# Four row tiles ahead of all weights, norm weight rows read from HBM, late row tiles through GpSimd's queue

## The chip, the cores and the metric

The kernel runs on the 8 cores of one Trainium2 chip. Every core runs the same program on its own data: one prompt of 2048 rows and 16 of the 128 sample rows. The metric is the device time in microseconds of the slowest core. TensorE (PE) multiplies, VectorE (DVE), ScalarE (ACT) and GpSimd (POOL) compute element by element, SyncE (SP) only issues transfers. GpSimd and ScalarE can issue transfers as well.

## The reference, cut to what matters

```
h = rmsnorm(x, g_mix);  proj = h @ w_in                # 1024 -> 3584 columns
a = proj[:, 0:512];  z = gelu(proj[:, 512:1536])       # z = u | v
gate_a, gate_b = sigmoid(proj[:, 1536:2560]), sigmoid(proj[:, 2560:3584])
pa = pool_mixer(a)     # per 128 columns: sums over windows of 2, 4, 8, 16 rows, mean - a, @ w_pool, * s_pool
v  = rmsnorm(v, g_v);  s = tril(w_s) @ v (chunks of 128 rows) + b_s;  sg = u * s
x  = x + (gate_a * (pa @ w_pool_out) + gate_b * (sg @ w_gmlp_out)) @ w_out
h2 = rmsnorm(x, g_ffn); x = x + (silu(h2 @ w_gate) * (h2 @ w_up)) @ w_down
y  = rmsnorm(x, g_final)
```

The outputs are y, the last 15 rows of a, the pool state of the samples, and v of the samples.

## The kernel before

The 2048 rows of a core are 16 row tiles of 128 rows and 1024 float32 columns (512 KB each in HBM), and the 16 sample rows are a 17th. They are read into the buffer X by `xload` (L614). All weights are packed into units of 128 x 1024 float32 values, 512 KB each in HBM. `load_unit` (L593) reads them through GpSimd's queue, which casts them to float16 on the way, into the ring buffer.

`norm` (L705) makes the normalised row tile. ScalarE squares and sums the rows, GpSimd raises the sum to the power -1/2 (L696), and VectorE (for tiles 0 and 1 half of it ScalarE) writes the float16 tile into hb, a buffer for two tiles. The tile is then transposed into hT. Tiles 0 to 7 are transposed on PE (L734) and copied out of PSUM; tiles 8 to 15 and the sample rows go by a transposing transfer on SP's queue (L722). With `late=True` (tiles 0 to 3) the tile is scaled by the row's factor alone and g_mix is multiplied in when it is copied out of PSUM, from its transposed form gT. Otherwise one VectorE instruction multiplies by factor and by gmix, g_mix repeated in all partitions.

The first part of the kernel, which alone is changed, runs over four blocks b of 512 rows (L870). A block has `a_stage` (L758, 4 groups of 128 columns), `chain` (L772, VectorE's window sums), `v_tile` (L811, one per row tile, with a norm of its own), and `u_stage` (L833, which also has the spatial product). It uses 12 weight units: a (4), v (4), u (4). Then follow the gates, the output product, and the two feed-forward parts, which are not changed.

The rows g_mix, g_v and b_s are needed in all 128 partitions. Before, they come as one row of 2048 values (`rowc`, L623), and PE repeats them by four float32 products with a row of ones, after which ScalarE and VectorE copy them out of PSUM into gmix, gv and bs_rep.

The order of the work on each engine is written by a planner, `schedule` (L232). It simulates the engines with a duration for each instruction and takes, for each engine, the operation that can start first, and among those the one with the lowest priority number. Transfers have a model of their own, `Traffic` and L301 to L311: a rate for each queue and a lead and a tail. The order is fixed when the program is built; on the chip every engine goes through its list in order, and waits on semaphores. `after=[...]` on a transfer makes it wait until another transfer has landed or another operation has ended. After planning, L1369 to L1392 fill gaps of PE's plan in the first 30 us with products that nobody reads (L1385, called filling products here).

Of the kernel before, what the change touches and what calls it, by code (L numbers as in the profile page):

```python
# [34 lines left out]
C_ID = 0  # L35
C_GT = C_ID + 128
C_STB = C_GT + 8
C_WS = C_STB + 1024
# [7 lines left out]
C_B0 = C_W00 + 4  # L46
C_GF = C_B0 + 4
C_GN = C_GF + 1024
C_ALL = C_GN + 1024

# [48 lines left out]
class Traffic:  # L99
# [9 lines left out]
    def steps(self, t, pend, until):  # L109
        while True:  # L110
            act = [q for q in pend if pend[q] and pend[q][0][1] <= t]
            nxt = min([x[0][1] for x in pend.values() if x and x[0][1] > t], default=float('inf'))
            rate = {q: (340.0 if t < 60000.0 else 300.0) if len(act) == 1 else (self.EARLY if t < 18000.0 else self.LATE)[q] for q in act}
            for q in act:
                nxt = min(nxt, t + pend[q][0][2] / rate[q])
            nxt = min(nxt, until)
            if nxt == float('inf'):
                return t
            for q in act:
                pend[q][0][2] -= (nxt - t) * rate[q]  # L120
# [21 lines left out]
class Prog:  # L142
# [89 lines left out]
    def schedule(self, bank_free0):  # L232
# [32 lines left out]
        while nleft:  # L265
# [35 lines left out]
            if o.dma is not None:  # L301
                if o.xbar:
                    o.done = o.end + 1900.0
                elif o.eng == 'act' and o.start < 20000.0:
                    o.done = o.end + 4100.0
                elif o.nbytes < 16384:
                    o.done = o.end + 3500.0
                elif o.eng == 'pool':
                    flow.add(o, 'pool', o.end, max(1600.0, 4900.0 - o.end), 900.0)
# [99 lines left out]
def build_nc():  # L409
    nc = bass.Bass("TRN2", target_bir_lowering=False)  # L410

    def din(name, shape):
        return nc.dram_tensor(name, list(shape), F32, kind="ExternalInput").ap()
# [20 lines left out]
    with es:  # L434
        def sb(name, shape, dt):
            return es.enter_context(nc.sbuf_tensor(name, list(shape), dt))
# [8 lines left out]
        junk = sb("junk", [128, XW], F16)  # L445
        idg = sb("idg", [128, 136], F32)
        ident_b = sb("ident_b", [128, 128], F16)
        wsbs = sb("wsbs", [128, 1024], F16)
        csm = sb("csm", [128, 80], F32)
        NCOL = 76  # L450
# [66 lines left out]
        def pt_():  # L517
            return PT()
# [94 lines left out]

        def xload(t, after=(), prio=None):  # L614
            prio = -10.0 + 0.1 * t if prio is None else prio
            if t < NT:
                o_ = dma('sp', X[:, XR(t), 0:D], xp[t * 128:(t + 1) * 128, :], 'x%d' % t, 524288, prio, after)
            else:
                o_ = dma('sp', X[:NSMP, XR(t), 0:D], xs[:, :], 'x%d' % t, 65536, prio, after)
# [19 lines left out]

        def cload(dst, c0, n, sem, prio, after):  # L640
            dma('sp', dst, cst[:, c0:c0 + n], sem, n * 512, prio, after=[after])
# [14 lines left out]
        memset('dve', AB[:, :, 0:32], 0.0)  # L656
        memset('dve', ones1[:, :], 1.0)
        vcopy(ident_b[:, :], ident_f[:, :], -5, 128)
        act(stmp[:, 0:1], mhalf[:, 0:1], AF.Square, -8.5)
        for j, (dst, nm) in enumerate(((gmix[:, 0:512], 'act'), (gmix[:, 512:1024], 'dve'), (gv, 'dve'),  # L660
                                       (bs_rep[:, :, :].rearrange("p g i -> p (g i)"), 'dve'))):
            pt = pt_()
            pr = -3.0
            mm(pt, lambda p: p[:, :], [(ones1[0:1, :], grow[0:1, 512 * j:512 * j + 512])], pr)
            if nm == 'act':
                act(dst, PV(pt, lambda p: p[:, :]), AF.Copy, pr)
            else:
                vcopy(dst, PV(pt, lambda p: p[:, :]), pr, 512, per=1.04)

# [35 lines left out]
        def norm(t, grep, prio, xbar=True, two=False, dst=None, late=False):  # L705
# [4 lines left out]
            if late:  # L710
                hw = 512 if t < 2 else 0
                if hw:
                    act(hbs[hi][:R, 0:hw], X[:R, XR(t), 0:hw], AF.Copy, prio, scale=r)
                ho = vts(hbs[hi][:R, hw:D], X[:R, XR(t), hw:D], r, None, ALU.mult, ALU.bypass, prio, D - hw)
            elif two:
                act(hbs[hi][:R, :], X[:R, XR(t), 0:D], AF.Copy, prio, scale=r)
                ho = vtt(hbs[hi][:R, :], hbs[hi][:R, :], grep[:R, :], ALU.mult, prio, D, per=0.52)
            else:
                ho = vstt(hbs[hi][:R, :], X[:R, XR(t), 0:D], r, grep[:R, :], ALU.mult, ALU.mult, prio, D)
            dst = hT[:, :, t * 128:t * 128 + R] if dst is None else dst  # L720
            if xbar:
                P.add('sp', lambda e: e.dma_start_transpose(out=dst, in_=hbs[hi][:R, :]),  # L722
                      reads=[hbs[hi][:R, :]], writes=[dst], dur=1220.0, lat=0.0, prio=-20.0,
                      dma='t%d' % hi, nbytes=330000).xbar = True
                return ho
            for h in range(2):
# [805 lines left out]
```

How the kernel before makes its waits and increments, by code:

```python
    def run(self, eng, e, sems):  # L391
        for o in self.order[eng]:
            for (sk, val) in o.waits:
                e.wait_ge(sems[sk], val)
            ins = o.fn(e)
            if o.dma is not None:
                ins.then_inc(sems[o.dma], 16)
            else:
                ins.then_inc(sems['E_' + eng], 1)
# [1008 lines left out]
            @block.sync  # L1408
            def _(e):
                P.run('sp', e, sems)
                for key in ('o0', 'o1', 'o2', 'o3', 'o4', 'o5', 'o6', 'q0', 'q1', 'q2', 'q3'):
                    e.wait_ge(sems[key], P.cnt[key])
```

## Time and profile before

| | |
|---|---|
| median of 3 runs | 757.73 us (757.55 to 758.4) |
| profiled execution | 757.22 us, span of its slowest core (core 0) 755.6 us |
| spans of cores 0 to 7 | 755.6, 754.2, 754.4, 754.2, 752.2, 753.8, 751.9, 754.4 us |
| PE busy | 739.2 us, 98% of the span |
| DVE, ACT, POOL busy | 548.6, 362.3, 98.7 us |

Times within the trace are microseconds from the start of the span. A row of the timeline has the start, the duration, the engine, the line, the operation, output and inputs, the shape, the count of instructions merged, and in brackets the idle time before and what ended it. A busy PE includes the filling products.

### The profile page before, as it was taken

What the parts mean: (1) busy time and instruction counts of PE and PEld (TensorE: products, weight loads), DVE (VectorE), ACT (ScalarE), POOL (GpSimd) and SP (SyncE); (2) the same over time, 40 slices, a digit from 0 to 9 for tenths busy, and PEclk for the clock granted to TensorE, in tenths of its full rate; (3) what the DMA queues carried; (4) which work ended last, traced back from release to release, by engine and by line L of the source; (5) the groups of instructions that cost most, each with busy time, mean ns of one, the idle gap of its engine ahead of it and who ended that gap; (6) DMA issues with size and microseconds to landing.
All of it is one profiled execution on the core that took longest, in us unless ns stands there. A gap on an engine that the chain in (4) does not pass through costs nothing.

```text
span 755.6 us, 14731 instructions; the slowest of 8 cores (751.9 to 755.6 us)
## 1 busy us (share of the span) xinstructions
PE 739.2 (98%) x4808; PEld 436.7 (58%) x4808; DVE 548.6 (73%) x1119; ACT 362.3 (48%) x788; POOL 98.7 (13%) x173
## 2 busy tenths in 40 slices
PE   8899899999999999999999999999999999999995
PEld 4554355666666664445666666666666654444543
DVE  3779898777777665787767676777667698766665
ACT  4695446454444446675555555555555521121212
POOL 3243232000000002222001000000000300000000
PEclk9999999999999999999999999999999999999998
DMA  8995437232313239677994232333222870623332
GB/s 191 207 293 80 58 60 121 36 43 54 43 29 40 59 95 266 112 117 104 230 270 83 42 46 41 56 64 50 43 43 43 110 185 2 221 89 137 130 97 112
DMA packets 53643, 77.46 MB, mean 103 GB/s; under 512 B 28736, under 2 KB 29120, under 8 KB 53551
## 3 DMA queue, kind: packets, MB, share of 16 engines
q0 software_dynamic: 15840, 28.84, 25.9%
q1 hardware_dynamic: 37294, 47.29, 22.1%
q8 instruction: 40, 0.66, 0.4%
q10 hardware_dynamic: 434, 0.38, 0.2%
q14 instruction: 35, 0.29, 0.1%
HBM read 82.04 MB, written 17.40 MB: 132 GB/s over the span
## 4 chain that ended last, share of the span: by engine, by line
PE 89%; DVE 3%; DMA 2%; issue 2%; ACT 2%; POOL 1%; SPq 0%; DVEq 0%; ACTq 0%; POOLq 0%
PE ps L529 87%; DMA X<-xp 1%; DMA hT<-hb 1%; PE ps L1070 1%; ACT junk L551 1%; PE ps L1385 1%; DVE hb L566 1%; POOL rs L696 1%; DVE actr L561 1%; PE ps L734 0%; ACT Fb L551 0%; DVE mrg L788 0%; DVE actr L566 0%; PE ps L848 0%; SPq L585 0%
## 5 line engine op out<-in xcount | busy, mean ns | idle before, releaser
L529 PE MATMUL ps<-hT,ring 128*128 128x384 f16 (+6 forms) x1428 | 231.9, 311 | 4.1 <-DMA hT<-hb 2.3
L561 DVE TENSOR_TENSOR Fb<-Fb,ps 128x344 f32<-128x344 f32 (+3 forms) x299 | 154.5, 531 | 52.0 <-PE ps L529 24.7
L529 PEld LDWEIGHTS ps<-hT,ring 128*128 128x128 f16 x1428 | 132.7, 98 | 83.0 <-issue 9.3
L551 ACT ACTIVATE Fb<-ps 128x384 f32<-128x384 f32 (+4 forms) x245 | 114.8, 475 | 122.7 <-PE ps L529 99.1
L561 DVE TENSOR_TENSOR X<-X,ps 128x512 f32<-128x512 f32 (+6 forms) x157 | 84.6, 546 | 53.1 <-PE ps L529 35.2
L551 ACT ACTIVATE Fb<-Fb 128x384 f32<-128x384 f32 (+2 forms) x174 | 85.9, 494 | 69.3 <-DVE Fb L561 67.4
L529 PE MATMUL ps<-actr,ring 128*128 128x344 f16 (+2 forms) x600 | 108.9, 309 | 0.1
L585 POOL DMA_DIRECT2D ring<-wpk x93 | 50.0, 545 | 310.3 <-PE ps L529 288.2
L529 PE MATMUL ps<-ring,mrg 128*128 128x512 f16 x360 | 81.4, 379 | 0.0
L529 PEld LDWEIGHTS ps<-actr,ring 128*128 128x128 f16 x600 | 57.5, 98 | 30.6 <-issue 0.5
L551 ACT ACTIVATE junk<-X 128x1025 f16<-128x1025 f32 (+3 forms) x40 | 41.5, 1038 | 46.8 <-DVE X L561 43.4
L529 PE MATMUL ps<-actr 128*128 128x384 f16 (+2 forms) x336 | 63.9, 324 | 0.0
L529 PEld LDWEIGHTS ps<-ring,mrg 128*128 128x128 f16 x360 | 35.1, 98 | 41.5 <-issue 0.4
L529 PE MATMUL ps<-actr,hb 128*128 128x384 f16 (+2 forms) x280 | 54.6, 319 | 0.0
L696 POOL TENSOR_TENSOR rs<-ss,mhalf 128x1 f32<-128x1 f32 (+1 forms) x51 | 39.0, 765 | 116.8 <-ACT junk L551 113.7
L529 PE MATMUL ps<-hT,X 128*128 128x512 f16 (+3 forms) x238 | 51.4, 338 | 0.0
L551 ACT ACTIVATE X<-ps 128x344 f32<-128x344 f32 (+2 forms) x87 | 38.1, 442 | 26.8 <-PE ps L529 23.1
L529 PE MATMUL ps<-hT,actr 128*128 128x384 f16 (+2 forms) x220 | 47.2, 337 | 0.0
L529 PEld LDWEIGHTS ps<-actr 128*128 128x128 f16 x336 | 32.8, 98 | 21.3 <-issue 0.2
L551 ACT ACTIVATE junk<-Fb 128x513 f16<-128x513 f32 (+2 forms) x25 | 19.2, 769 | 40.4 <-DVE Fb L561 36.8
L529 PEld LDWEIGHTS ps<-actr,hb 128*128 128x128 f16 x280 | 27.4, 98 | 16.2
L529 PE MATMUL ps<-hT,hb 128*128 128x384 f16 (+3 forms) x188 | 36.5, 321 | 0.0
(178 smaller groups left out, 795.0 us busy)
## 6 DMA issues: line engine op xcount, KB each, us to landing
ring<-wpk POOLq DMA_DIRECT2D x93, 256.0 KB, 4.8
X<-xp SPq DMA_DIRECT2D x25, 512.0 KB, 7.4
x1d<-X SPq DMA_DIRECT2D x16, 512.0 KB, 13.0
Fb<-x1d SPq DMA_DIRECT2D x8, 512.0 KB, 4.1
yp<-Fb SPq DMA_DIRECT2D x8, 512.0 KB, 2.8
hT<-wpk POOLq DMA_DIRECT2D x8, 256.0 KB, 11.6
X<-x1d SPq DMA_DIRECT2D x4, 512.0 KB, 4.3
actr<-x1d SPq DMA_DIRECT2D x4, 512.0 KB, 3.9
```

The costliest lines, as they stand in the source:

```text
L529: ins = e.matmul(out=ap, lhsT=l, rhs=rr, start=(start and i == 0), stop=(stop and i == len(pairs) - 1), skip_group_check=skip)
L551: return e.activation(out=P.r(out), in_=P.r(in_), func=func, scale=scale, **kw)
L561: return P.add(eng, lambda e: e.tensor_tensor(out=P.r(out), in0=P.r(a), in1=P.r(b), op=op), reads=[a, b], writes=[out], dur=vdur(n, per), ...
L566: return P.add('dve', lambda e: e.scalar_tensor_tensor(out=P.r(out), in0=P.r(a), scalar=sc, in1=P.r(b), op0=op0, op1=op1), reads=rd, write ...
L585: return P.add(q, lambda e: e.dma_start(out=out, in_=in_), reads=[in_], writes=[out], dur=(560.0 if q == 'pool' else 400.0), lat=0.0, prio ...
L696: P.add('pool', lambda e: e.tensor_tensor(out=rs[:R, k:k + 1], in0=ss[:R, k:k + 1], in1=mhalf[:R, 0:1], op=ALU.pow), reads=[ss[:R, k:k + 1 ...
L1070: ins = e.matmul(out=o_, lhsT=l, rhs=r, start=(m_ == 0), stop=(m_ == len(terms[dd]) - 1))
L1385: ins = e.matmul(out=PS[7][:, :], lhsT=z[:, 512:640], rhs=z[:, 0:512], start=True, stop=True)
```

## The change

- Only the four row tiles 0 to 3 are issued at once on SP's queue; all a and v units wait until row tile 1 has landed.
- g_mix, g_v and b_s are stored in HBM repeated 128 times and are read by transfers (1 MB in all); the four products, their copies and `rowc` are gone. b_s is cast by one VectorE copy.
- The causal mask comes first on GpSimd's queue; gT moves into csm.
- Row tiles 8 to 11 wait for unit u1 only and stay on SP's queue. Row tiles 12 to 15, the sample rows and the constants of the samples (C_STB, C_WP, C_SEL) move to GpSimd's queue, behind row tile 9 or 11.
- Tiles 4 to 7 are normalised with `late=True`. Where `late` is set, VectorE now does the whole scaling and both halves of the copy out of PSUM, which ScalarE shared before.
- The planner's rates, leads and tails for transfers are altered, and the filling products are counted from 0.95 us on instead of 2.0 us.

```diff
-            rate = {q: (340.0 if t < 60000.0 else 300.0) if len(act) == 1 else ...
+            rate = {q: (300.0 if not 8000.0 < t < 60000.0 else 340.0) if len(act) == 1 else ...
...
-                    o.done = o.end + 1900.0
+                    flow.add(o, 'sp', o.end, 100.0, 1070.0)
...
-                    flow.add(o, 'sp', o.end, 1300.0, 900.0)
+                    flow.add(o, 'sp', o.end, 1300.0, 1200.0 if 600.0 < o.end < 3000.0 else 900.0)
...
-        dma('act', idg[:, :], cst[:, C_ID:C_ID + 136], 'c0', 69632, -10.1)
-        dma('act', grow[0:1, 0:2048], rowc[:, :], 'c1', 8192, -10)
-        dma('act', csm[:, 0:76], cst[:, C_SM:C_SM + 76], 'c3', 38912, -8.95)
-        for t in range(2):
+        for t in range(4):
             xload(t)
-        for t in range(2, 4):
-            xload(t)
+        dma('act', ident_f[:, :], cst[:, C_ID:C_ID + 128], 'c0', 65536, -10.1)
+        dma('act', csm[:, 0:84], cst[:, C_SM:C_SM + 84], 'c3', 43008, -10.0)
+        dma('pool', mask, cst[:, C_MASK:C_MASK + 128], 'c7', 65536, -11.0)
         wd_ = {}
         for g in range(4):
-            wd_[('a', g)] = load_unit(('a', g), 8 + g, 0.1 + 0.01 * g)
+            wd_[('a', g)] = load_unit(('a', g), 8 + g, 0.1 + 0.01 * g, [x_dma[1]])
         for k in range(4):
-            wd_[('v', k)] = load_unit(('v', k), k, 0.2 + 0.01 * k)
+            wd_[('v', k)] = load_unit(('v', k), k, 0.2 + 0.01 * k, [x_dma[1]])
...
-        cload(mask, C_MASK, 128, 'c7', -9.63, wd_[('a', 3)])
-        cload(mrg[:, o + 1536:o + 2048], C_WS, 512, 'c8', -9.62, wd_[('v', 0)])
-        cload(mrg[:, o + 512:o + 1536], C_STB, 1024, 'c9', -1, wd_[('u', 3)])
-        cload(mrg[:, o + 2048:o + 2560], C_WP, 512, 'c10', -1, wd_[('u', 3)])
-        cload(mrg[:, o + 2560:o + 2688], C_SEL, 128, 'c11', -1, wd_[('u', 3)])
-        for t in range(4, 12):
-            if t not in x_dma:
-                xload(t, after=[wd_[('u', 1 if t < 8 else 2)]])
+        cload(mrg[:, o + 1536:o + 2048], C_WS, 512, 'c8', -9.26, wd_[('v', 3)])
+        cload(gv, C_GM + 1024, 512, 'c1', -9.25, wd_[('v', 3)])
+        cload(bs_raw, C_GM + 1536, 512, 'c12', -9.24, wd_[('v', 3)])
+        cload(gmix, C_GM, 1024, 'c13', -9.05, wd_[('u', 1)])
+        for t in range(8, 12):
+            xload(t, after=[wd_[('u', 1)]])
...
-        memset('dve', ones1[:, :], 1.0)
...
-        for j, (dst, nm) in enumerate(((gmix[:, 0:512], 'act'), (gmix[:, 512:1024], 'dve'), (gv, 'dve'),
-                                       (bs_rep[:, :, :].rearrange("p g i -> p (g i)"), 'dve'))):
-            ...
-            mm(pt, lambda p: p[:, :], [(ones1[0:1, :], grow[0:1, 512 * j:512 * j + 512])], pr)
-            ...
+        vcopy(bs_rep[:, :, :].rearrange("p g i -> p (g i)"), bs_raw, 7.5, 512)
...
-                hw = 512 if t < 2 else 0
-                if hw:
-                    act(hbs[hi][:R, 0:hw], X[:R, XR(t), 0:hw], AF.Copy, prio, scale=r)
-                ho = vts(hbs[hi][:R, hw:D], X[:R, XR(t), hw:D], r, None, ALU.mult, ALU.bypass, prio, D - hw)
+                ho = vts(hbs[hi][:R, :], X[:R, XR(t), 0:D], r, None, ALU.mult, ALU.bypass, prio, D)
...
-                    if h:
-                        for k in range(4):
-                            act(dst[:, 4 + k, :], PV(pt, ...), AF.Copy, prio, scale=gT[:, 4 + k, :], n=R)
-                    else:
-                        vtt(dst[:, 0:4, :], src, gT[:, 0:4, :].to_broadcast([128, 4, R]), ALU.mult, prio, 4 * R)
+                    vtt(dst[:, 4 * h:4 * h + 4, :], src, gT[:, 4 * h:4 * h + 4, :].to_broadcast([128, 4, R]), ALU.mult, prio, 4 * R)
...
-                    h_op[t] = norm(t, gmix, base - 95.0 + 0.1 * (t % 4), xbar=b > 1)
+                    h_op[t] = norm(t, gmix, base - 95.0 + 0.1 * (t % 4), xbar=b > 1, late=b < 2)
             if b == 1:
                 for t in range(12, NT):
-                    xload(t, after=[h_op[t - 8]])
+                    xload(t, after=[h_op[t - 8], x_dma[9]], prio=0.5 + 0.01 * t, q='pool')
+                cload(mrg[:, o + 512:o + 1536], C_STB, 1024, 'c9', 0.7, x_dma[11], q='pool')
+                cload(mrg[:, o + 2048:o + 2560], C_WP, 512, 'c10', 0.71, x_dma[11], q='pool')
+                cload(mrg[:, o + 2560:o + 2688], C_SEL, 128, 'c11', 0.72, x_dma[11], q='pool')
                 if b == 1:
-                    xload(NT, after=[h_op[7]])
+                    xload(NT, after=[h_op[7], x_dma[9]], prio=0.49, q='pool')
...
-        t_ = 2000.0
+        t_ = 950.0
...
-                n_ = int((gap - 200.0) / (300.0 if t_ < 5000.0 else 235.0)) if gap > 700.0 else 0
+                n_ = int((gap - 200.0) / (420.0 if t_ < 2000.0 else 235.0)) if gap > 700.0 else 0
```

## Rows read from the trace of the kernel before

**Rows 1.** Busy us of each engine (instructions) by stretch, core 0; then granted clock, DMA share, GB/s.
```profile
20.00:40.00 20.00, 17.93 (x141) 11.04 (x139) 15.81 (x39) 12.97 (x35) 7.40 (x10) 1.00 0.92 222
...
36.90:124.00 87.10, 84.21 (x507) 41.87 (x505) 75.00 (x133) 52.20 (x116) 30.89 (x41) 0.98 0.59 118
...
160.00:240.00 80.00, 80.00 (x551) 53.69 (x549) 59.18 (x130) 39.80 (x89) 5.30 (x10) 1.00 0.26 40
```
**Rows 2.** Timeline of PE, core 0.
```profile
5.93 5.48 PE L529 MATMUL ps<-Fb,mrg 1*128 1x512 f32 x6
11.34 1.03 PE L734 MATMUL ps<-ident_b,hb 128*128 128x128 f16 x8
...
28.79 5.34 PE L529 MATMUL ps<-ring,hT 128*128 128x512 f16 x24
...
36.87 1.89 PE L529 MATMUL ps<-ring,hT 128*128 128x512 f16 x8
...
78.20 8.75 PE L529 MATMUL ps<-hT,ring 128*128 128x512 f16 x32 [2.30 <-DMA hT<-hb]
...
124.08 0.39 PE L848 MATMUL ps<-wsbs,mrg 128*128 128x128 f16 x4
```
**Rows 3.** Timeline of PE, core 7: first products of tile 4, last spatial products.
```profile
38.04 1.89 PE L529 MATMUL ps<-ring,hT 128*128 128x512 f16 x8
...
122.60 0.39 PE L848 MATMUL ps<-wsbs,mrg 128*128 128x128 f16 x4
```
**Rows 4.** Timeline of PE, core 6: the same two, and the a products of block 2.
```profile
34.63 1.89 PE L529 MATMUL ps<-ring,hT 128*128 128x512 f16 x8
...
74.35 7.07 PE L529 MATMUL ps<-hT,ring 128*128 128x512 f16 x32 [0.80 <-DMA hT<-hb]
...
121.67 0.39 PE L848 MATMUL ps<-wsbs,mrg 128*128 128x128 f16 x4
```
**Rows 5.** Row tile 1 and unit a0: ns of the issue, its start, us from issue to landing.
```profile
L585 SPq DMA_DIRECT2D X<-xp x1: 412/412/412, 1.5 to 1.5; - x1
DMA to landing us min/median/max: 5.8/5.8/5.8
...
L585 POOL DMA_DIRECT2D ring<-wpk x1: 664/664/664, 1.5 to 1.5; - x1
DMA to landing us min/median/max: 10.4/10.4/10.4
```
**Rows 6.** The same for unit v3 and for unit u0.
```profile
L585 POOL DMA_DIRECT2D ring<-wpk x1: 587/587/587, 5.3 to 5.3; - x1
DMA to landing us min/median/max: 20.0/20.0/20.0
...
L585 POOL DMA_DIRECT2D ring<-wpk x1: 577/577/577, 28.8 to 28.8; - x1
DMA to landing us min/median/max: 5.2/5.2/5.2
```
**Rows 7.** Chain of waits, core 0, start, length, what: row tile 11, the last of blocks 0 to 2.
```profile
44.23 10.79 DMA X<-xp
```
**Rows 8.** Waits of SP's queue in the first 100 us: total, times, longest.
```profile
SPq L394 <- DVE hb L566: 41.3, 11, 9.0
```
**Rows 9.** VectorE in norm: combined form, scaling alone, the two copies out of PSUM (min/median/max ns).
```profile
L566 DVE SCALAR_TENSOR_TENSOR hb<-X,rs,mrg 128x1024 f16<-128x1024 f32 x10 | 12.7, 1279 | 2.7 <-DMA hT<-hb 1.9 <-POOL rs L696 0.8
...
16.24 0.75 DVE L572 TENSOR_SCALAR hb<-X,rs 128x1024 f16<-128x1024 f32 x1
...
L577 DVE COPY hT<-ps x4: 418/421/424, 36.2 to 43.0; 128x512 f16<-128x512 f16 x4
...
L561 DVE TENSOR_TENSOR hT<-ps,idg x4: 692/692/693, 12.5 to 22.0; 128x512 f16<-128x512 f16 x4
```
**Rows 10.** Timeline of POOL: a root beside an idle VectorE, and one beside a busy one.
```profile
14.37 0.55 POOL L696 TENSOR_TENSOR rs<-ss,mhalf 128x1 f32<-128x1 f32 x1 [5.08 <-ACT junk L551]
...
36.89 1.32 POOL L696 TENSOR_TENSOR rs<-ss,mhalf 128x1 f32<-128x1 f32 x1 [1.60 <-ACT junk L551]
```

More of the change, by code:

```diff
@@ L35 @@
 C_ID = 0
-C_GT = C_ID + 128
-C_STB = C_GT + 8
+C_STB = C_ID + 128
 C_WS = C_STB + 1024
@@ L46 @@
 C_B0 = C_W00 + 4
-C_GF = C_B0 + 4
+C_GT = C_B0 + 4
+C_GF = C_GT + 8
 C_GN = C_GF + 1024
-C_ALL = C_GN + 1024
+C_GM = C_GN + 1024
+C_ALL = C_GM + 2048
 def unit_list():
@@ L112, in steps @@
             nxt = min([x[0][1] for x in pend.values() if x and x[0][1] > t], default=float('inf'))
-            rate = {q: (340.0 if t < 60000.0 else 300.0) if len(act) == 1 else (self.EARLY if t < 18000.0 else self.LATE)[q] for q in act}
+            rate = {q: (300.0 if not 8000.0 < t < 60000.0 else 340.0) if len(act) == 1 else (self.EARLY if t < 18000.0 else self.LATE)[q] for q in act}
             for q in act:
@@ L308, in schedule @@
                 elif o.eng == 'pool':
-                    flow.add(o, 'pool', o.end, max(1600.0, 4900.0 - o.end), 900.0)
+                    flow.add(o, 'pool', o.end, max(1600.0, 5000.0 - o.end), 900.0)
                 else:
-                    flow.add(o, 'sp', o.end, 1300.0, 900.0)
+                    flow.add(o, 'sp', o.end, 1300.0, 1200.0 if 600.0 < o.end < 3000.0 else 900.0)
             else:
@@ L445, in build_nc @@
         junk = sb("junk", [128, XW], F16)
-        idg = sb("idg", [128, 136], F32)
+        ident_f = sb("ident_f", [128, 128], F32)
         ident_b = sb("ident_b", [128, 128], F16)
         wsbs = sb("wsbs", [128, 1024], F16)
-        csm = sb("csm", [128, 80], F32)
+        csm = sb("csm", [128, 84], F32)
         NCOL = 76
@@ L612, in build_nc, with xload @@
         x_dma = {}
-        def xload(t, after=(), prio=None):
+        def xload(t, after=(), prio=None, q='sp'):
             prio = -10.0 + 0.1 * t if prio is None else prio
             if t < NT:
-                o_ = dma('sp', X[:, XR(t), 0:D], xp[t * 128:(t + 1) * 128, :], 'x%d' % t, 524288, prio, after)
+                o_ = dma(q, X[:, XR(t), 0:D], xp[t * 128:(t + 1) * 128, :], ('x%d' if q == 'sp' else 'y%d') % t, 524288, prio, after)
             else:
-                o_ = dma('sp', X[:NSMP, XR(t), 0:D], xs[:, :], 'x%d' % t, 65536, prio, after)
+                o_ = dma(q, X[:NSMP, XR(t), 0:D], xs[:, :], ('x%d' if q == 'sp' else 'y%d') % t, 65536, prio, after)
             x_dma[t] = o_
-        dma('act', idg[:, :], cst[:, C_ID:C_ID + 136], 'c0', 69632, -10.1)
-        dma('act', grow[0:1, 0:2048], rowc[:, :], 'c1', 8192, -10)
-        dma('act', csm[:, 0:76], cst[:, C_SM:C_SM + 76], 'c3', 38912, -8.95)
-        for t in range(2):
+        for t in range(4):
             xload(t)
-        for t in range(2, 4):
-            xload(t)
+        dma('act', ident_f[:, :], cst[:, C_ID:C_ID + 128], 'c0', 65536, -10.1)
+        dma('act', csm[:, 0:84], cst[:, C_SM:C_SM + 84], 'c3', 43008, -10.0)
+        dma('pool', mask, cst[:, C_MASK:C_MASK + 128], 'c7', 65536, -11.0)
         wd_ = {}
         for g in range(4):
-            wd_[('a', g)] = load_unit(('a', g), 8 + g, 0.1 + 0.01 * g)
+            wd_[('a', g)] = load_unit(('a', g), 8 + g, 0.1 + 0.01 * g, [x_dma[1]])
         for k in range(4):
-            wd_[('v', k)] = load_unit(('v', k), k, 0.2 + 0.01 * k)
+            wd_[('v', k)] = load_unit(('v', k), k, 0.2 + 0.01 * k, [x_dma[1]])
         xg = {4: ('v', 1), 5: ('v', 1), 6: ('v', 2), 7: ('v', 3)}
@@ L638, in build_nc, with cload @@
             wd_[('u', g)] = load_unit(('u', g), 4 + g, 0.3 + 0.01 * g, [x_dma[4 + g]])
-        def cload(dst, c0, n, sem, prio, after):
-            dma('sp', dst, cst[:, c0:c0 + n], sem, n * 512, prio, after=[after])
-        cload(mask, C_MASK, 128, 'c7', -9.63, wd_[('a', 3)])
-        cload(mrg[:, o + 1536:o + 2048], C_WS, 512, 'c8', -9.62, wd_[('v', 0)])
-        cload(mrg[:, o + 512:o + 1536], C_STB, 1024, 'c9', -1, wd_[('u', 3)])
-        cload(mrg[:, o + 2048:o + 2560], C_WP, 512, 'c10', -1, wd_[('u', 3)])
-        cload(mrg[:, o + 2560:o + 2688], C_SEL, 128, 'c11', -1, wd_[('u', 3)])
-        for t in range(4, 12):
-            if t not in x_dma:
-                xload(t, after=[wd_[('u', 1 if t < 8 else 2)]])
+        def cload(dst, c0, n, sem, prio, after, q='sp'):
+            dma(q, dst, cst[:, c0:c0 + n], sem, n * 512, prio, after=[after])
+        cload(mrg[:, o + 1536:o + 2048], C_WS, 512, 'c8', -9.26, wd_[('v', 3)])
[4 more added lines that the diff above has]
+            xload(t, after=[wd_[('u', 1)]])
         zm = memset('dve', actr[:, 0, 1408:2048], 0.0, -6.0)
@@ L723, in norm @@
                       reads=[hbs[hi][:R, :]], writes=[dst], dur=1220.0, lat=0.0, prio=-20.0,
[L724 removed]
+                      dma='t%d' % hi, nbytes=250000).xbar = True
                 return ho
@@ L1521 @@
             "xp": x_prompt[c], "xs": np.ascontiguousarray(x_sample[c * NSMP:(c + 1) * NSMP, 0, :]),
-            "st": stc, "cst": cc, "rowc": rowc, "wpk": wpk,
+            "st": stc, "cst": cc, "wpk": wpk,
         })
```

17 lines of the change are left out of this document (3 added, 14 removed).

## The prediction

> **What bounds the kernel now.** I read the busy time by stretch first. From 160 to 240 us PE is busy for all of its time at granted clock 1.00 [rows 1], and so, but for a few us, up to the end. What happens before about 125 us is therefore passed on one to one: whatever time PE's last spatial product of block 3 gains, the kernel gains. I take that product as the landmark. It stands at 124.08 us on core 0, which is the slowest [rows 2], at 122.60 on core 7 [rows 3] and at 121.67 on core 6 [rows 4]. From there to the end of the span are 755.6 - 124.1 = 631.5, 754.4 - 122.6 = 631.8 and 751.9 - 121.7 = 630.2 us.
>
> Then the timeline of PE, for what delays the landmark. The reader is to see two marks. The products of row tile 4 (the first of block 1) start at 36.87 on core 0, when the a and v products of block 0 are done. The a products of block 2 start at 78.20 after 2.30 us of waiting for a transposed row tile, and their 32 products then take 8.75 us, where core 6 needs 7.07 [rows 2, 4]: 1.7 us more, with a lower granted clock after the wait.
>
> Does a gain at the first mark reach the landmark? The cores answer that. Core 7 comes to its first mark at 38.04, 3.4 us behind core 6 (34.63), but to the landmark only 0.9 us behind [rows 3, 4]. From mark to landmark are 87.2 us on core 0, 87.0 on core 6 and 84.6 on core 7. An early start is mostly eaten by something that stands at a fixed time. The chain of waits names it: row tile 11, issued at 44.23, landing at 55.0 [rows 7], and from it the squares, roots, scaling and transposing transfers to the wait at 78.20. So there are two limits: the start of block 1, and the arrival of row tiles 8 to 11. The transfer engines are full meanwhile (share 0.92 from 20 to 40 us, [rows 1]), and SP's queue waited 41.3 us for VectorE [rows 8]: in its order tiles 12 to 15 stand ahead of 8 to 11, behind the scaling of tiles 4 to 7.
>
> **The change part by part.** *Row products.* Eight float32 records go; the first six stand from 5.93 to 11.34, ahead of the first transposes [rows 2]. Their place is empty then, not used: the a products need unit a0, which now waits for tile 1. That landed at 1.5 + 5.8 = 7.3 us [rows 5]; with 0.6 us of issue and u0's 5.2 us to landing [rows 6], a0 lands at 13.1 instead of 1.5 + 10.4 = 11.9 [rows 5]. The later seven units took (25.3 - 11.9)/7 = 1.9 us each before, with two row tiles beside them (v3: 5.3 + 20.0 = 25.3, rows 5, 6). At the rate below 524 KB alone in the queues take 1.9 us too, or 1.6 if that rate contains gaps. So v3 lands between 24.3 and 26.4: 25 us, unchanged. Tiles 2 and 3 come earlier and their norms are then over when weights land; the a products (block 0: 7 us) run as units arrive, and the v products of block 0, done at 34.0 before [rows 2], end about 1.7 us after v3, at 27.
>
> *The first mark.* It needs tile 4 in hT. Tile 4 still waits for v1 and lands near 27.7 (before: at u0's issue at 28.8, rows 6, at the latest). Square 1.25, root 0.55 plus hand-over, scaling 0.75 [rows 9, 10], transposes and copy: 5 us. Mark at 32.6, or 31 to 35. That is 4.3 us earlier on core 0, 2.0 on core 6, 5.4 on core 7. By the least remainder of [rows 3], 84.6 us, the landmark follows at 117.2; by the greatest, 87.2, at 119.8.
>
> *The second limit.* Up to the landing of tile 11, 16 row tiles, 12 units (524 KB each) and 0.44 MB of constants were read: 15.1 MB in the 53.9 us since 1.1 us, 0.28 MB per us. Now tiles 12 to 15 are behind (-2.10 MB) and the repeated rows are ahead (three of 262 KB with the spatial weights, gmix 524 KB; 1.05 MB more than before): 14.07 MB, so tile 11 lands at 1.1 + 50.2 = 51.3, 3.7 us earlier. If tiles 12 and 13 on the other queue share with 10 and 11, 1.05 MB or 3.7 us come back and nothing is gained; if the queues run without the hole that SP's waits leave, 2 us more are gained. I take 3.7, the price of the bytes. The wait at 78.20 moves to 74.5; from there to the landmark are 124.1 - 78.2 = 45.9 us, without the slow clock 44.2: 118.7. If that slow clock comes back, 120.4.
>
> *VectorE.* For each of tiles 4 to 7 a combined form (1.28) and one copy (0.42) become a scaling (0.75) and two products (0.69 each) [rows 9]: +0.43 us, +1.7 for four. In block 0 two halves of scaling and four more copies of 0.69 come from ScalarE, while three copies of the repeated rows go: about +1 us, at a time when VectorE waits for weights anyway. Between the marks VectorE was busy for 75.0 of 87.1 us [rows 1]; now 76.5 of about 86. It has room in the sum but not everywhere, since its order is fixed: nothing at the low end, 1.7 us at the high end. ScalarE's load falls. I put 0.3 us.
>
> *GpSimd's queue.* Nine transfers more at 0.58 us [rows 6] are 5.2 us. It was busy 30.9 of 87.1 us between the marks [rows 1], so they fit. But each waits in line: tiles 12 to 15 for tile 9 and for the scaling of tiles 4 to 7, the constants for tile 11, and the roots of `v_tile` and `norm` stand behind them. Here the planned order must hold; nothing to 8 us, taken as 0. A root of 0.55 us already takes 1.32 while VectorE is busy [rows 10].
>
> The Trainium skill (SBUF — State Buffer, section "Who interferes with whom") says that a DVE copy, cast or `tensor_scalar` in a two-port mode locks the port that GpSimd needs for writing descriptors; it speaks against this change, which makes four more `tensor_scalar` and issues nine more transfers on GpSimd. By that rule each meeting would cost at most one scaling, 0.75 us, some 3 us in all on GpSimd. The trace's issues of 0.58 and 0.59 us show no such wait; the rule alters neither the sum nor a chance.
>
> *The rest.* The filling products move 1 us forward and change only what PE does while it has nothing to do. The mask and gT cost nothing new.
>
> **Sum.** The later of 117.2 to 119.8 and 118.7, with 0.3 us: landmark at 119.0 us, against 124.1 on core 0 and 122.4 on the middle core. With 631.5 us behind it, the span is 750.5; the slower tail of some cores adds 0.3. The profiled execution lay 757.22 - 755.6 = 1.6 us over its span: 752.4. The median of the runs lies 0.5 us over the profiled one: 752.9 us, a gain of 4.8.
>
> **Rivals.** (A) *The added bytes eat it.* Tiles 10 and 11 share with the GpSimd queue, tile 11 lands at 55.0 as before, and the wait at 78.20 stays. Only core 0's lower clock or part of the start is gained, 1 to 2 us: 756.3. For it: the full engines [rows 1]. Against: SP's queue had 41.3 us of waits [rows 8] that tiles 8 to 11 no longer stand behind. The Trainium skill (DMA: Bandwidth & Descriptors, "Issuing engines are not separate DMA queues") says that all queues end on the same 16 engines, so that moving a transfer gains its place in the order only; the trace's share of 0.92 agrees.
>
> (B) *VectorE becomes the bound* between the marks: its added work shows in full and once more in PE's waits for it. 2 to 2.5 us of the gain go: 755.2. For it: busy for 86% of that stretch [rows 1]. Against: core 7 did the same work in 84.6 us.
>
> (C) *GpSimd's queue blocks* (the other side). If tile 9 lands later than planned, the issue of tile 12 holds up every root behind it, VectorE waits for the roots, PE for VectorE. Tile 9 is at 13.0 MB, about 47.6 us by the rate above. Each us of lateness beyond the slack is lost; it decides from 6 us on (the gain of 4.8 and the bound of 1.5 us). With 8 us: 761.
>
> (D) *More is gained*: the first mark at 31 us and no wait at block 2. The landmark at 31 + 84.6 = 115.6: 749.5.
>
> **Chances.** Forecast 0.48 (its own range 751 to 755), A 0.16, B 0.14, C 0.11, D 0.11. What a measurement can tell from no change is 0.2%, 1.5 us, so faster is below 756.2. Of the forecast, B and D all is faster except 0.03; of A a third: 0.75. Same: 0.03 and half of A, 0.13; slower: C and what is left of A, 0.12. The range reaches from D to A's upper end: 749.0 to 757.5.
>
> **What would show it.** First products of tile 4 at 31 to 35 us on all cores. Landing of tile 11 at about 51. The a products of block 2 at about 74.5 with little wait and no lower clock after it. The last spatial product at about 119, all cores within 2 us. 630 to 632.5 us from there to the end. It is wrong if roots on GpSimd stand behind its issues for more than 2 us, if tile 11 lands at 55, or if new waits of PE for VectorE show up between 40 and 120 us. It is also wrong if the stretch behind the landmark changes, for which nothing here speaks.

## The result and the profile after

The changed kernel takes 767.98 us (765.79 to 769.24, 4 runs) against 758.07 us (757.55 to 758.94, 4 runs) of the kernel before: 1.0127 times as long, 95% interval 1.0114 to 1.014, 9.9 us between the medians. The forecast was 752.9 us with a range to 757.5. A ratio with an interval in brackets is below always that of a kernel to the kernel before, measured beside it.

| | before | after |
|---|---|---|
| span of the slowest core | 755.6 us (core 0) | 767.9 us (core 7) |
| last spatial product, cores 0 to 7 | 124.1, 122.6, 122.0, 122.0, 121.8, 122.7, 121.7, 122.6 | 132.5, 131.7, 132.5, 130.4, 128.2, 130.0, 130.2, 136.7 |
| from there to the end of the span | 630.2 to 632.4 us on all cores | 631.2 to 633.0 us on all cores |
| PE, DVE busy | 739.2, 548.6 us | 737.4, 549.7 us |

The stretch behind the landmark has kept its length, to within 1 us. So the loss lies before the last spatial product. Further rows of the kernel after are of core 7 where no other core is named.

The timeline of PE at the two marks and at the landmark (columns as in [rows 2]):

```profile
14.66 1.05 PE L527 MATMUL ps<-hT,ring 128*128 128x128 f16 x16 [2.32 <-DMA ring<-wpk]
...
28.08 3.61 PE L527 MATMUL ps<-ring,hT 128*128 128x512 f16 x16 [1.30 <-DMA ring<-wpk]
...
34.67 1.89 PE L527 MATMUL ps<-ring,hT 128*128 128x512 f16 x8 [0.24 <-DVE hT L559]
...
39.89 5.30 PE L527 MATMUL ps<-hT,ring 128*128 128x512 f16 x16 [2.44 <-DMA ring<-wpk]
...
75.58 0.85 PE L527 MATMUL ps<-hT,ring 128*128 128x16 f16 x16 [5.92 <-ACT mrg L549]
77.60 0.36 PE L527 MATMUL ps<-hT,ring 128*128 128x16 f16 x8 [1.17 <-ACT mrg L549]
78.70 0.36 PE L527 MATMUL ps<-hT,ring 128*128 128x16 f16 x8 [0.74 <-ACT Fb L549]
79.18 3.57 PE L527 MATMUL ps<-ring,hT 128*128 128x512 f16 x8
84.47 1.87 PE L825 MATMUL ps<-wsbs,mrg 128*128 128x128 f16 x16 [1.71 <-ACT junk L549]
86.13 2.79 PE L527 MATMUL ps<-ring,hT 128*128 128x512 f16 x8
...
136.68 0.39 PE L825 MATMUL ps<-wsbs,mrg 128*128 128x128 f16 x4
```

The reader is to see the first products of tile 4 at 34.67, where [rows 3] have 38.04: the early start is there. But from that mark to the landmark are 102.0 us instead of 84.6. Of the 17.4 us more, 10.4 are idle time (12.2 us of waits in the trace, 1.8 before) and about 5 are a lower clock, 1.7 of them at 39.9 us and 3.4 between 79 and 89. Eight 128x512 products take 3.57 and 2.79 us where [rows 2] have 1.89. Sixteen spatial products take 1.87 where the same sixteen take 1.05 in an undisturbed stretch of the first experiment, and the sixteen products at 39.89 take 5.30 against 3.61 at 28.08. The other 1.9 us I can't assign. The windows show the clock in the column behind the brackets of POOL (columns as in [rows 1]):

```profile
40.00:45.00 5.00, 5.00 (x16) 1.90 (x15) 0.84 (x5) 0.60 (x1) 0.00 (x0) 0.66 0.90 153
60.00:65.00 5.00, 5.00 (x25) 2.29 (x24) 0.09 (x1) 1.23 (x3) 1.55 (x3) 1.00 1.13 98
65.00:70.00 5.00, 4.66 (x22) 1.93 (x20) 0.00 (x0) 0.85 (x1) 0.00 (x0) 1.00 1.10 208
75.00:80.00 5.00, 2.27 (x35) 1.49 (x36) 5.00 (x9) 5.00 (x12) 1.74 (x3) 0.50 0.25 47
```

From 60 to 70 us VectorE stands still while PE still runs on what it has, and from 75 to 80 us PE itself is busy less than half of the time at 0.50 (1.2 GHz). The timeline of VectorE names the wait, and the chain of waits (start, length, what) names what is behind it:

```profile
58.82 1.27 DVE L564 SCALAR_TENSOR_TENSOR hb<-X,rs,mrg 16x1024 f16<-16x1024 f32 x1
72.11 1.28 DVE L564 SCALAR_TENSOR_TENSOR hb<-X,rs,mrg 128x1024 f16<-128x1024 f32 x1 [12.03 <-DMA hT<-hb]
```
```profile
12.68 9.37 DMA ring<-wpk
22.12 7.69 DMA X<-xp
...
30.34 9.42 DMA ring<-wpk
39.89 5.30 PE ps L527 x16
...
54.19 17.83 DMA hT<-hb
```

Two things stand there. Row tile 4, issued at 22.12, lands at 29.8; unit u0 waits for it, is issued at 30.34 and lands after 9.4 us, not 5.2 as in [rows 6]. And a transposing transfer of SP's queue, issued at 54.2 (row tile 8, which VectorE wrote at 52.8), lands after 17.8 us; hb has room for two tiles and the sample rows are in the other half (58.82 above), so VectorE can't write tile 9. The view of the hT tile on SP's queue shows both transfers that are hit, that of tile 8 and that of the sample rows (columns: ns of the issue, first and last start), first of after, then of the same core before:

```profile
L704 SPq DMA_TRANSPOSE hT<-hb x2: 1142/1234/1325, 54.2 to 60.2; - x2
DMA to landing us min/median/max: 12.5/15.2/17.8
```
```profile
L722 SPq DMA_TRANSPOSE hT<-hb x9: 1217/1232/2017, 56.1 to 84.6; - x9
DMA to landing us min/median/max: 3.1/3.3/4.2
```

What is on the engines meanwhile? GpSimd's queue, with the late tiles (timeline of POOL):

```profile
51.34 0.53 POOL L583 DMA_DIRECT2D X<-xs  x1
...
52.62 0.58 POOL L583 DMA_DIRECT2D X<-xp  x1
53.22 1.32 POOL L681 TENSOR_TENSOR rs<-ss,mhalf 128x1 f32<-128x1 f32 x1
54.51 1.62 POOL L583 DMA_DIRECT2D X<-xp  x3
...
57.29 1.63 POOL L583 DMA_DIRECT2D mrg<-cst  x3
```

How do the two queues share the engines? First the size of the packets. One transposing transfer of a row tile with the engines to itself (ninth experiment below, core 5, DMA view from 54 to 56 us: packets, MB, share of 16 engines):

```profile
q1 hardware_dynamic: 1056, 0.26, 69.2%
```

That is 0.26 MB, a tile of 128 x 1024 values of 2 bytes, in 1056 packets of 256 bytes or less. Now core 4 of the kernel after, from 55 to 60 us, where both queues have work (q0 is GpSimd's, q1 is SP's):

```profile
q0 software_dynamic: 355, 1.30, 91.7%
q1 hardware_dynamic: 357, 0.09, 12.4%
```

GpSimd's queue passes 355 packets of 3.7 KB in the time in which SP's passes 357 small ones. One for one: where packets take turns, a transfer cut into 256-byte packets gets a fifteenth of the bytes. The Trainium skill (DMA: Bandwidth & Descriptors, "Queues, rings and completion order") says that each DMA engine goes round between its queues packet by packet; the counts of this stretch agree.

Turns are not the whole of it. On core 7 the counts are 106 and 618 from 55 to 60 us, and from 58 to 62 us both queues together move only 46 GB/s. In the sixth experiment GpSimd's queue passes 335 packets from 54 to 58 us and SP's none, though a transposing transfer was issued at 53.6. What slows the small packets beyond the turns is not shown by any run.

The collision slows the other side too. ScalarE, which goes through its list in order, waited for row tile 13, which landed at 69.1, 14.6 us after its issue:

```profile
69.14 1.06 ACT L549 ACTIVATE junk<-X 128x1025 f16<-128x1025 f32 x1 [7.92 <-DMA X<-xp]
```

So on core 7 a second path is nearly as late: the root that VectorE needs for its work at 73.32 was done at 71.8, as ScalarE stood behind tile 13. With a short transposing transfer alone this core would have gained only some 1.5 us there (an estimate from these rows). On cores 2 and 3 ScalarE did not wait for a row tile, and VectorE stood still for 9.9 and 9.3 us all the same; of core 2:

```profile
68.16 1.28 DVE L564 SCALAR_TENSOR_TENSOR hb<-X,rs,mrg 128x1024 f16<-128x1024 f32 x1 [9.93 <-DMA hT<-hb]
```

### The profile page after: what moved, and what is told of

Read it like the earlier page. It is cut to its first block, busy times and chain, and to the rows that moved or that the text cites. A ratio compares the mean times of both kernels' runs of the same rounds, so it can differ in the third digit from the quotient of the medians.

```text
span 767.9 us, 14708 instructions; the slowest of 8 cores (760.0 to 767.9 us)
## 1 busy us (share of the span) xinstructions
PE 737.4 (96%) x4812; PEld 435.8 (57%) x4812; DVE 549.7 (72%) x1124; ACT 355.6 (46%) x765; POOL 102.6 (13%) x182
## 4 chain that ended last, share of the span: by engine, by line
PE 87%; DMA 7%; DVE 2%; issue 1%; ACT 1%; POOL 1%; DVEq 0%; SPq 0%; ACTq 0%; POOLq 0%
PE ps L527 85%; DMA ring<-wpk 2%; DMA hT<-hb 2%; DMA X<-xp 2%; PE ps L1050 1%; ACT junk L549 1%; DVE actr L559 1%; PE ps L825 0%; DMA hT<-Fb 0%; POOL rs L681 0%; ACT Fb L549 0%; POOL ring L583 0%; DVE X L559 0%; PE ps L1065 0%; DVE mrg L564 0%
## 5 line engine op out<-in xcount | busy, mean ns | idle before, releaser
L549 ACT ACTIVATE Fb<-ps 128x384 f32<-128x384 f32 (+5 forms) x245 | 115.2, 475 | 128.2 <-PE ps L527 108.5
L549 ACT ACTIVATE Fb<-Fb 128x384 f32<-128x384 f32 (+2 forms) x174 | 85.9, 494 | 69.1 <-DVE Fb L559 67.2
L583 POOL DMA_DIRECT2D ring<-wpk x93 | 51.5, 560 | 323.2 <-PE ps L527 290.2
L681 POOL TENSOR_TENSOR rs<-ss,mhalf 128x1 f32<-128x1 f32 (+1 forms) x51 | 36.5, 716 | 112.8 <-ACT junk L549 111.7
```

Source lines behind the costliest of these rows:

```text
L549: return e.activation(out=P.r(out), in_=P.r(in_), func=func, scale=scale, **kw)
L583: return P.add(q, lambda e: e.dma_start(out=out, in_=in_), reads=[in_], writes=[out], dur=(560.0 if q == 'pool' else 400.0), lat=0.0, prio ...
L681: P.add('pool', lambda e: e.tensor_tensor(out=rs[:R, k:k + 1], in0=ss[:R, k:k + 1], in1=mhalf[:R, 0:1], op=ALU.pow), reads=[ss[:R, k:k + 1 ...
```

## The experiments

Theory 1: the transfers on GpSimd's queue slow the transposing transfers. Theory 2: the added 1 MB of rows delays units and tiles. Theory 3: GpSimd's queue as such is the matter (its own descriptor path, roots behind its issues).

### Late tiles back on SP's queue (e1_sp_queue)

```diff
-  xload(t, after=[h_op[t - 8], x_dma[9]], prio=0.5 + 0.01 * t, q='pool')   # 12 to 15, xs, constants
+  xload(t, after=[h_op[t - 8]])                                            # and constants behind u3
```


> The changed kernel with one part undone: row tiles 12 to 15, the sample rows and the sample constants are back on SP's queue with their old waits. Theory 1 (a transposing transfer on SP's queue takes turns, packet by packet, with the GpSimd queue; the change put 2.9 MB of large packets there just as the transposes of tiles 8 and the sample rows start, and these took 17.8 and 12.5 us instead of about 3): transposing transfers at 3 to 5 us, no 12 us wait of VectorE between 60 and 72 us, median 755 to 759 us, about 10 us under the changed kernel. Theory 2 (the 1 MB more of rows and the later weights cause the loss): the wait moves elsewhere, 764 us or more.

Measured 761.7 us, 1.0052 [1.0035, 1.007]. On its slowest core the transposing transfers were short:

```profile
L707 SPq DMA_TRANSPOSE hT<-hb x5: 1126/1237/1326, 60.7 to 74.8; - x5
DMA to landing us min/median/max: 2.3/3.1/3.2
```

The stall is gone, and 0.75 points of the loss (5.7 us) with it; the landmarks are at 122.6 to 127.1. The time lies between what the two theories expected: 4 us of loss remain. On that core the u units landed at 39.4, 43.3, 45.8 and 48.7 and PE waited at 39.6:

```profile
39.61 3.55 PE L527 MATMUL ps<-hT,ring 128*128 128x512 f16 x8 [3.06 <-DVE wsbs L559]
```

### GpSimd's queue alone (e2_pool_only)

The kernel before, with only tiles 12 to 15, the sample rows and the constants on GpSimd's queue, as in the change.

> The kernel before with that one part of the change alone: tiles 12 to 15, the sample rows and constants on GpSimd's queue, behind tile 9 or 11; weights at once, row products and planner's rates as before. Theory 1: the first transposing transfers meet the same packets, take over 10 us, and the kernel is slower by 6 to 12 us: 764 to 770. Theory 2: no loss, 756 to 759 us, as tiles 8 to 11 are earlier.

Measured 761.46 us, 1.0053 [1.0034, 1.0073]: the sign is right, the size half of what was expected. The longest transposing transfer on the slowest core took 9.7 us and VectorE waited 5.61 us:

```profile
64.63 1.28 DVE L566 SCALAR_TENSOR_TENSOR hb<-X,rs,mrg 128x1024 f16<-128x1024 f32 x1 [5.61 <-DMA hT<-hb]
```

### The same transfers from ScalarE's queue (e3_act_queue)

```diff
-  q='pool'
+  q='act'        # tiles 12 to 15, xs and the three constants
```


> The changed kernel with the same transfers at the same point, but issued from ScalarE's hardware queue instead of GpSimd's. If the loss comes from two queues taking turns by packets (theory 1), the transposing transfers stall as before, over 10 us, 765 to 771 us. If it comes from GpSimd writing descriptors late or being blocked by VectorE (theory 3), they land in 3 to 5 us and the time is 755 to 760 us.

Measured 763.88 us, 1.0083 [1.0059, 1.0107], from two runs: between what the two theories expected. A transposing transfer of 14.2 us is there with no GpSimd in it. The transposing transfers of the slowest core, then the queues from 54 to 62 us (q10 is ScalarE's):

```profile
L704 SPq DMA_TRANSPOSE hT<-hb x5: 1141/1241/1774, 52.0 to 73.2; - x5
DMA to landing us min/median/max: 3.1/3.1/14.2
```
```profile
q10 hardware_dynamic: 774, 2.33, 91.0%
q1 hardware_dynamic: 595, 0.15, 12.2%
```

So a second queue is enough to make such a transfer long, it need not be GpSimd's. But the stall is not the same: the transfers were issued from 48.8 us on, VectorE waited 4.0 us behind the long one and not 12.0, and the engines moved 311 GB/s from 54 to 62 us where core 7 of the changed kernel moved 98 to 107 from 55 to 65. Theory 3 falls for the long transfer; whether GpSimd's queue adds to the stall stays open.

### Rows cut into smaller pieces (e4_small_packets)

The changed kernel, with each tile on GpSimd's queue read as two transfers, of the even and of the odd pieces of 128 columns (512 bytes each in HBM).

> The changed kernel with row tiles 12 to 15 read through GpSimd's queue in pieces of 128 columns (512 bytes) instead of 4 KB rows: the same bytes, eight times the packets if a packet is a piece. Theory 1 (turns by packets): a transposing transfer of 800 packets gets by while 800 small packets pass, some 0.4 MB, so it lands in 4 to 8 us and the time falls to 757 to 763 us. Rival (the bytes or the full engines alone slow them): as the changed kernel or slower, 767 to 772 us.

Measured 762.03 us, 1.0067 [1.0023, 1.0112]; the transposing transfers of the slowest core took 7.6, 8.3 and 10.8 us. But the packets did not become small (and a transposing transfer is 1056 of them, not 800). From 60 to 65 us, core 5:

```profile
q0 software_dynamic: 350, 1.17, 85.3%
```

That is 3.3 KB per packet. The pieces are joined into packets almost as long as before (3.7 KB), so this run can't say whether smaller ones would help. Why the stall was shorter stays open; the starts moved too.

### Rows repeated by PE again, late tiles on SP's queue (e5_sp_and_pe_rows)

The first experiment, with `rowc`, the four float32 products and their copies of the kernel before instead of the 1 MB of repeated rows.

> The changed kernel with two parts undone: late tiles and sample constants on SP's queue, and g_mix, g_v and b_s repeated by PE's four products instead of 1 MB of reads. What is left of the change are the four row tiles ahead of the weights, the scaling of tiles 4 to 7 and the planner's numbers. Theory 2b (the 4 us that stay when the late tiles are back on SP come from the 1 MB, read on SP's queue between 28 and 40 us in turns with the u units, which land at 39.4 to 48.7 us there and at 34.0 to 45.9 before): u0 at about 35, median 754 to 757.5 us. Rival (the late start of the weights or VectorE's added work causes them): 760 to 763 us.

Measured 758.9 us, 1.0007 [0.9993, 1.002]. On its slowest core the u units landed at 37.0, 40.0, 43.2 and 46.7, 2 to 3 us sooner than in the first experiment. That is the second part of the loss, 0.45 points. The time lies between the two expected ranges, and u0 was to land at 35: not all of the delay of the u units is the rows.

### Rows repeated by PE, GpSimd's queue kept (e6_pe_rows)

> The changed kernel with only the rows undone: late tiles stay on GpSimd's queue. If the two losses add up (late tiles 6 us, rows 4 us), 763 to 765 us, with transposing transfers of over 8 us. If the late tiles then land before the first transpose and the stall goes, 757 to 759 us.

Measured 758.89 us, 1.0022 [1.0004, 1.0039]: the lower range, but without its condition, as the stall did not go. On the slowest core tiles 12 to 15 were issued at 47.9 to 51.5 (after: 52.6 to 55.6) and landed by 58.9 (after: 73.4). Tile 12 was 5.7 us ahead of the first transposing transfer (53.6), in the changed kernel 1.6 us (54.2). That transfer took 9.1 us, the second 5.2, both landing some 4 us after tile 15; the later ones took 3.1 to 3.3. VectorE waited 3.05 us:

```profile
L713 SPq DMA_TRANSPOSE hT<-hb x6: 1130/1220/1640, 53.6 to 72.5; - x6
DMA to landing us min/median/max: 3.1/3.2/9.1
```

The same queue and the same bytes on it, 4 us sooner against the transposes: half the transfer time, a quarter of the wait. The parts of the change are not additive.

### Repeated rows from HBM alone (e7_hbm_rows_only)

The kernel before with the repeated rows read from HBM (spatial weights and their order as before) and tiles 4 to 7 scaled late.

> The kernel before with the rows read from HBM, and with tiles 4 to 7 scaled late, as they cannot wait for gmix; weights at once, late tiles on SP's queue. Theory 2b: the u units land 3 to 5 us later, the first a products may start earlier as no row products stand ahead, together 758 to 762 us. Rival (the bytes are free, the row products were the cost, as I predicted): 752 to 756 us.

Measured 758.1 us, 1.0002 [0.999, 1.0014]. The first mark was at 33.7 to 35.8 us, 1 to 3 us sooner than before on six of eight cores, and the time is the same, at the lower edge of what theory 2b expected. Of core 7 mark and landmark:

```profile
34.93 1.24 PE L528 MATMUL ps<-ring,hT 128*128 128x512 f16 x5
...
120.31 0.39 PE L840 MATMUL ps<-wsbs,mrg 128*128 128x128 f16 x4
```

That core gained 2.3 us at the landmark (span 751.1 us). Core 3 reached it only at 125.04 (span 755.9), after waits of 1.15 us for a u unit and 2.55 us for VectorE. Without the collision some cores gain, and the slowest, which sets the time, does not.

### Tiles first alone (e8_tiles_first_only)

```diff
-  wd_[('a', g)] = load_unit(('a', g), 8 + g, 0.1 + 0.01 * g)
+  wd_[('a', g)] = load_unit(('a', g), 8 + g, 0.1 + 0.01 * g, [x_dma[1]])   # the v units too
```


> The kernel before with the a and v units waiting for row tile 1 and nothing else changed. a0 lands at 14.5 us instead of 11.9, v3 about as before. If the late start costs nothing, 757 to 758 us; if it is a part of the loss, 759 to 761 us; if the earlier tiles 2 and 3 help, 755 to 757 us.

Measured 757.84 us, 0.9994 [0.9981, 1.0006]: no difference. The landmarks are at 120.3 to 122.7; seven cores waited 0.3 to 1.6 us for a u unit between 42 and 47 us.

### Late tiles on GpSimd's queue, behind the transposes (e9_behind_transposes)

```diff
-  xload(t, after=[h_op[t - 8], x_dma[9]], prio=0.5 + 0.01 * t, q='pool')
+  xload(t, after=[h_op[t - 8], P.ops[h_op[11].i + 1]], prio=0.5 + 0.01 * t, q='pool')   # the constants too
```
The cut is shortened: these calls also move to block 2 of the program. The sample rows are read as in the change.

> The changed kernel with one thing moved: row tiles 12 to 15 and the constants of the samples stay on GpSimd's queue, but are issued only when the transposing transfer of tile 11 has landed. Theory 1 (the stall is made by packets of another queue that are on the engines at the same time): the transposing transfers of tiles 8 to 11 then take 2 to 5 us each instead of 17.8 and 12.5, VectorE's idle 12 us goes, the landmark falls from 136.7 to 124 to 129 us and the time lies at 758.5 to 763, as with the transfers on SP's queue (761.7); only the transposing transfers of tiles 12 to 15 may wait for their rows. Rival (what costs is that the transfers stand on GpSimd's queue at all: its issues, its cast path, roots held up behind waits): 764 or more, with idle time of VectorE or PE behind roots. The time can also be lost again if tile 12 lands after 85 us.

Measured 762.08 us, 1.0071 [1.005, 1.0093]. With the first experiment this is the run that decides: the changed kernel, the row tiles on GpSimd's queue, only not at that time. The slowest core, 45 to 76 us:

```profile
L704 SPq DMA_TRANSPOSE hT<-hb x5: 1147/1228/1327, 52.9 to 71.5; - x5
DMA to landing us min/median/max: 2.3/3.1/3.2
```

No stall of VectorE is left there. The collision has moved to where the tiles now land: the transposes of tiles 12 and 13 (issued at 83.8 and 86.2, beside weight units) took 5.4 and 3.9 us, and PE waited for one:

```profile
89.36 3.61 PE L527 MATMUL ps<-ring,hT 128*128 128x512 f16 x16 [1.59 <-DMA hT<-hb]
```

The landmark there is at 125.0. What is left of the loss is of the size of the first experiment's, which has the same repeated rows. What the two runs show is that it matters which transfers are in flight together; they don't tell turns by packets from any other way in which one queue can hold up another.

### Tiles first and late scaling, nothing else (e10_tiles_first_late_scaling)

> The kernel before with two parts of the change: a and v units wait for row tile 1, and tiles 4 to 7 are normalised with the row factor alone, g_mix being multiplied in by VectorE on the copy out of PSUM. The rows are still repeated by PE, and everything stays on SP's queue in the order of before. If the early gain at the first mark is worth anything by the time of the last spatial product, 755.5 to 757; if something at a fixed later time eats it, 757.5 to 758.5.

Measured 758.59 us, 1.0019 [1.0005, 1.0033]: not faster. The first mark was at 34.9 to 37.9 us, no sooner than before on most cores.

### Planner's numbers of before (e11_planner_before)

The fifth experiment's kernel with the old rates, leads and tails and the old filling products.

> The changed kernel with SP's queue for the late tiles, the rows repeated by PE (that one took 758.9) and now also the planner's numbers and the filling products of before. What is left of the change: four tiles first, the mask first on GpSimd's queue, tiles 8 to 11 behind unit u1, tiles 4 to 7 scaled late. If the planner's new numbers cost something by themselves, 757.0 to 758.2, faster than 758.9 by 0.7 us or more; if the last us is lost in the order of the tiles, 758.5 to 759.5.

Measured 758.7 us, 1.0013 [1.0002, 1.0024], against 1.0007 with the new numbers: the intervals overlap, the new numbers cost nothing that can be seen. No version beats the kernel before.

## Why the prediction was wrong

**The stretch behind the landmark.** Predicted 630 to 632.5 us, measured 631.2 to 633.0. Right but for 0.5 us on one core, and so the landmark was the right thing to follow.

**The first mark.** Predicted 32.6 (31 to 35), measured 34.67 on core 7 and 31.7 to 34.7 on all. Right in sign and size, though by a longer way: a0 landed at 14.5 us instead of 13.1, v3 at 28.6 instead of 25, row tile 4 at 29.8 instead of 27.7. The wait for tile 1 cost a0 2.6 us instead of 1.2, and the seven units behind it took (28.6 - 14.5)/7 = 2.0 us each where 1.6 to 1.9 had been put.

**GpSimd's queue: "nothing to 8 us, taken as 0".** This is the step that failed. I looked for the harm on GpSimd (roots behind issues) and for bytes, and not at who else has packets on the engines at 54 to 72 us: the transposing transfers of tile 8 and of the sample rows, cut some 15 times finer than the rest. The term measured 5.7 us by the undoing (first experiment, 0.75 points) and 0.53% as the part alone (second). On core 7 it shows as 12.0 us of VectorE's time, and from that 9.5 us of PE's waits (5.92, 1.17, 0.74, 1.71) with the clock at half speed behind them. That it is the meeting in time, and not GpSimd's queue as such, is shown by moving the same transfers in time on the same queue (sixth, which also drops the repeated rows, 9.1 us; ninth, 3.2 us), and that a second queue is enough by the third. The prediction also took it that moving a transfer gains its place in the order only: with the same bytes on the same engines the move cost 5.7 us, so it changes the shares as well. Packet turns as the mechanism rest on counts of the trace (355 to 357 on core 4) that other stretches don't repeat; the run that was to vary the packet size did not vary it. So that step is read from the trace, not shown by an experiment, and it is not the whole.

**That the first mark passes on to the landmark by 84.6 to 87.2 us.** This term was mis-sized too. In the first experiment, which has no stall, the early marks (32.0 to 34.3) are followed by 90.5 to 93.3 us on every core. The prediction named row tile 11 as what eats an early start, but left out the u units, which block 1 needs directly behind its first products. u0 was priced at its old 5.2 us; in the changed kernel it took 9.4 and landed at 39.7, where core 0 before has 34.0. PE waited 2.44 us there and then ran at granted clock 0.66. Taking the repeated rows out again brought u0 2.4 us forward and the time down by 0.45 points (fifth). In experiments 5, 7 and 8 the remainder is 85 to 90 us, near the old one; but there the marks come only about 1 us earlier (34 to 37 us against 34.6 to 38.0), and the slowest core gains nothing. No combination of the parts that ran was faster than the kernel before, let alone by 4.8 us.

**The second limit.** Tile 11 was to land at 51.3 by the bytes, 3.7 us sooner; it landed at 54.3, though none of tiles 12 to 15 had landed before it. So the 14.07 MB took 53.2 us, 0.26 MB per us instead of 0.28: the rate was taken over from a different mixture. Why it was lower is not shown; the rates of the DMA view don't settle it, as they count a weight unit by the 256 KB that are written, half of what is read. The late landing is nearly the premise of rival A. Its 756.3 is too low as well: in the first experiment, without the stall, the time was 761.7.

**VectorE's added work**, put at 0.3 us: busy 549.7 against 548.6 us in all, unseen in the time. The port rule of the Trainium skill (SBUF — State Buffer, "Who interferes with whom") was judged to have no effect, from issues of 0.58 and 0.59 us. The trace of the changed kernel agrees with the rule instead: four issues of weight units take 0.97 to 1.03 us, and each has a scaling of VectorE beside it, as here.

```profile
31.70 1.02 POOL L583 DMA_DIRECT2D ring<-wpk  x1
31.85 0.75 DVE L570 TENSOR_SCALAR hb<-X,rs 128x1024 f16<-128x1024 f32 x1 [3.28 <-POOL rs L681]
```

The other issues of weight units take 0.53 to 0.58. That is 0.45 us for each meeting, some 2 us of GpSimd's time in all, where the prediction's estimate by the rule was 3. It does not touch the late tiles, whose issues take 0.53 to 0.58 us.

**The rivals.** C had the sign and the queue, and was wrong in place and reason: before the root at 49.6 us POOL had been idle for 11.6 us, and no root of that stretch waited behind an issue for more than 2 us. Its 761 us was too small as well. The chance of slower, 0.12, covered only that mechanism (by the prediction's own parts it is 0.14, and that of the same time 0.11, not 0.13). B, VectorE as the bound, did not come: it idled 12 us. D's early mark did come on some cores (31.7 us), D's time on none.

**How the 1.27% adds up.** GpSimd's queue alone +0.53, rows with late scaling alone +0.02, tiles first alone -0.06: +0.49 in sum, each known to 0.1 or 0.2. The other 0.8 points are not in these parts alone. Part of them is their meeting: with the repeated rows tiles 12 to 15 are issued from 52.6 us on instead of 47.9 (sixth experiment), into the transposes. Taking out either part gives much back (the late tiles' queue 0.75, the rows 1.05 points), both 1.2. The rest of the change (the mask first, tiles 8 to 11 behind u1, block 0's scaling on VectorE) never ran alone; with both parts out it is 0.07 to 0.13% slower than before.

## What to carry to other kernels

Before a transfer is moved to another queue, list which transfers are in flight on the others at that time and how finely they are cut; here the one in small packets, the transposing transfer, lost its share to the large ones, and it was safe when it was kept apart by order: in the same queue, or by a wait for the last small one. Ask as well which engine stands in line behind the large ones. An early start is worth only what the next data in line allows: follow the landing of every unit that the stretch needs, not the last tile alone. And parts that each cost nothing can meet: price the moved schedule as a whole.

## What the runs showed of the hardware

- A transposing transfer of 128 x 1024 two-byte values is 1056 packets of 256 bytes or less, 0.26 MB. It lands after 2.2 to 3.5 us where no row tiles are on a second queue (first and ninth experiment, all cores, up to 70 us). Beside row tiles on a second queue the longest of each core took 13.5 to 17.8 us in the changed kernel, 8.9 to 9.6 us on seven cores of the sixth experiment (5.5 on the eighth), and 10.8 to 14.2 us beside ScalarE's queue in the third.
- The throughput falls in some of these meetings and not in others, and why is open. Core 7 of the changed kernel moved 98 GB/s from 60 to 65 us (above). Core 4 moved this from 55 to 60 us, and core 4 of the third experiment, with ScalarE's queue, this from 54 to 62:

```profile
55.00:60.00 5.00, 5.00 (x25) 2.28 (x24) 1.31 (x2) 2.30 (x5) 2.76 (x4) 1.00 1.05 281
54.00:62.00 8.00, 7.99 (x29) 3.10 (x28) 6.48 (x13) 5.05 (x10) 1.59 (x3) 0.67 1.03 311
```

- Reading rows in pieces of 512 bytes through GpSimd's queue did not make packets small (3.3 KB each).
- The issue of a weight unit on GpSimd took 0.97 to 1.03 us beside a scaling of VectorE (TENSOR_SCALAR, 0.75 us), and 0.53 to 0.58 without.
- The granted clock was 0.66 from 40 to 45 us, after 2.44 us of idle PE, and 0.50 from 75 to 80 us, after 5.9 us: about 5 of the 17.4 us lost between mark and landmark are the clock.
